# The low parts of the first three query weights are subtracted on GpSimd in place of VectorE

## What is computed

```
x  = x + g1 * _rms(mix_x @ w_out, norm_post_mix)
h2 = _modulate(_rms(x, norm_pre_ffn), sh2, sc2)
q  = h2 @ peer_w_query              # 512 x 1024 @ 1024 x 2048
s1 = q[..., :128] @ keys1.T         # per head; s2 with the other half
v1, i1 = top_k(s1, 16) ...          # candidates, top 16 of 256, softmax
out = x + g2 * _rms(sum over the picked experts of gelu(h2 . u) * v, norm_post_ffn)
```

## Time and profile before

| | us |
|---|---|
| median of 3 runs | 1504.64 (1502.85 to 1504.99) |
| the profiled execution | 1502.96 |
| its span | 1501.2 |
| PE busy | 1479.3 (99%) |
| DVE busy | 1242.2 (83%) |
| ACT busy | 578.0 (39%) |
| POOL busy | 438.7 (29%) |

### The profile page before, as it was taken

One profiled execution on the slowest core, in us unless ns is written; L12 is line 12 of the kernel. 1 busy time (PEld: TensorE's weight loads), 2 busy tenths in 40 slices (PEclk: granted clock), 3 DMA queues, 4 the chain that ended last, 5 costly groups with the idle time before them and its releaser, 6 DMA issues.

```text
span 1501.2 us, 21716 instructions
## 1 busy us (share of the span) xinstructions
PE 1479.3 (99%) x8085; PEld 1305.6 (87%) x8085; DVE 1242.2 (83%) x2364; ACT 578.0 (39%) x869; POOL 438.7 (29%) x373
## 2 busy tenths in 40 slices
PE   8999999999999999999999999999999999999998
PEld 3887888788999999999999999988888888888886
DVE  3888758776899998999999955698888888888886
ACT  4432143622333334344444443343333333333333
POOL 1130000010578886432222201322222222222210
PEclk9999999999999999999999999999999999999999
DMA  9775113134358896799999999999999999999983
GB/s 387 267 285 183 57 57 112 43 98 155 135 197 303 288 312 216 264 337 359 372 363 372 371 324 353 388 412 363 377 354 379 386 369 381 385 362 368 367 320 129
DMA packets 149158, 433.49 MB, mean 289 GB/s; under 512 B 13408, under 2 KB 46432, under 8 KB 146272
## 3 DMA queue, kind: packets, MB, share of 16 engines
q1 hardware_dynamic: 73296, 203.91, 37.2%
q0 software_dynamic: 42048, 153.11, 27.9%
q10 hardware_dynamic: 33744, 75.64, 13.3%
HBM read 378.08 MB, written 54.53 MB: 288 GB/s over the span
## 4 chain that ended last, share of the span: by engine, by line
PE 73%; DVE 19%; DMA 3%; issue 2%; ACT 1%; POOL 0%; SPq 0%; ACTq 0%; DVEq 0%
PE ps L1688 22%; PE ps L1690 22%; PE ps L1689 22%; PE ps L2078 3%; DVE rows L1485 2%; DMA part_w<-w_ada 2%; DMA ada_w<-w_ada 2%; DVE part_acc L1114 1%; DVE ps L1517 1%; DVE ps L1521 1%; DVE picks L1523 1%; PE ps L2018 1%; DVE tv L1451 1%; DVE tv L1454 1%; DVE ws_lo L1081 1%
## 5 line engine op out<-in xcount | busy, mean ns | idle before, releaser
L1688 PE MATMUL ps<-hT_hi,ws_hi 128*128 128x384 f32 (+1 forms) x976 | 341.2, 350 | 2.7 <-POOL ws_lo L632 1.5
L1690 PE MATMUL ps<-hT_hi,ws_lo 128*128 128x384 f32 (+1 forms) x976 | 335.2, 343 | 0.0
L1689 PE MATMUL ps<-hT_lo,ws_hi 128*128 128x384 f32 (+1 forms) x976 | 335.1, 343 | 0.0
L1688 PE MATMUL ps<-vs_hi,coef_hi 128*128 128x512 f32 x768 | 299.0, 389 | 0.8 <-DVE coef_lo L1647 0.8
L1690 PE MATMUL ps<-vs_hi,coef_lo 128*128 128x512 f32 x768 | 298.8, 389 | 0.0
L1689 PE MATMUL ps<-vs_lo,coef_hi 128*128 128x512 f32 x768 | 298.8, 389 | 0.0
L970 ACT ACTIVATE vs_hi<-blk_raw 128x1024 fp32r<-128x1024 f32 x128 | 135.7, 1060 | 284.8 <-PE ps L1690 282.2
L640 POOL DMA_INDIRECT rows<-u_nat,ids x128 | 142.7, 1115 | 300.6 <-DVE sp_act L1485 293.0
L640 POOL DMA_INDIRECT rows<-v_nat,ids x128 | 127.1, 993 | 332.2 <-DVE ps L1605 300.4
L1644 DVE TENSOR_TENSOR vs_lo<-blk_raw,vs_hi 128x1024 fp32r<-128x1024 f32 x128 | 156.6, 1224 | 67.7 <-ACT vs_hi L970 66.7
L916 ACT ACTIVATE ws_hi<-blk_raw 128x1024 fp32r<-128x1024 f32 x102 | 108.1, 1060 | 245.9 <-PE ps L1690 242.4
(11 more groups left out here) (319 smaller groups left out, 2232.0 us busy)
## 6 DMA issues: line engine op xcount, KB each, us to landing
blk_raw<-u_t SPq DMA_DIRECT2D x128, 512.0 KB, 5.8
blk_raw<-v_nat SPq DMA_DIRECT2D x128, 512.0 KB, 7.1
g_dram<-g_buf ACTq DMA_DIRECT2D x128, 192.0 KB, 4.9
w_dram<-w_stage SPq DMA_DIRECT2D x48, 512.0 KB, 8.5
grp_g<-g_dram ACTq DMA_DIRECT2D x15, 1536.0 KB, 9.9
grp_w<-w_dram ACTq DMA_DIRECT2D x15, 1536.0 KB, 25.8
part_w<-w_ada POOLq DMA_DIRECT2D x32, 512.0 KB, 5.9
raw<-w_in SPq DMA_DIRECT2D x20, 512.0 KB, 6.6
```

What stands on the lines that cost most here:

```text
L1688: pe.matmul(o, lh, rh, start=start, stop=False, skip_group_check=True)
L1689: pe.matmul(o, lh, rl, start=False, stop=False, skip_group_check=True)
L1690: return pe.matmul(o, ll, rh, start=False, stop=stop, skip_group_check=True)
```

## The change

Units 28, 29 and 30 have their low parts subtracted on GpSimd. The three calls of `rest_unit` on DVE are gone. GpSimd gets three subtractions, each behind a wait for the rounded high part and for the count of low parts before it; they stand behind the memsets and ahead of `apply_gain(2, ...)`. DVE gets one wait, ahead of `rest_unit(31)`, for the third of them, so that the count stays in order.

```diff
+POOL_UNITS = (28, 29, 30)
...
+            for n in POOL_UNITS:
+                pool.wait_ge(split_hi, n + 1)
+                pool.wait_ge(split_lo, n)
+                pool.tensor_tensor(ws_lo[slot(n)][:], raw[:, n % RAW, :], ws_hi[slot(n)][:].bitcast(F32),
+                                   ALU.subtract).then_inc(split_lo, 1)
             pool.wait_ge(split_used, 31)
             pool.wait_ge(gg_step, 4)
             apply_gain(2, gg_last)
...
-                if tb >= 2:
-                    rest_unit(26 + tb)
                 sum_x(tb)
...
-                if m == 3:
-                    rest_unit(30)
...
             dve.wait_ge(gg_step, 4)
             for m in range(2 * PH):
+                if m == 3:
+                    dve.wait_ge(split_lo, POOL_UNITS[-1] + 1)
                 if m >= 3:
                     rest_unit(28 + m)
                     take_pair(m - 3)
```

## The result

The changed kernel takes 1506.03 us in the median, the kernel before, run beside it, 1502.66 us (18 runs each; the three runs known before gave 1504.64). The ratio is 1.0023 with a 95% interval of 1.0016 to 1.0031, so the kernel became 2.4 to 4.7 us slower; 3.8 us was forecast. One disturbed execution of the changed kernel (2111 us, mean granted clock 0.654) and one of the kernel before in a later set (2870 us) are left out of the comparisons; the median of the other 17 is 1505.94 us.

The account below looks back on a forecast made before the run. The bound was taken as the chain of waits ending on PE (73%) and DVE (19%), with PE waiting for the normalization. 1.1 + 1.95 + 0.75 = 3.8 us on 1504.64 gave 1508.4, range 1506.0 to 1511.2.

Parts of the forecast that it names:

- the holds: Between 270 and 290 us, DVE instructions with two SBUF inputs wait until POOL's subtraction ends; 3.8 us in sum.
- the clock: Rival: PE's clock falls to 1.2 GHz in a 3.6 us gap before the matmul of ones, 2.3 us more; chance 0.14.
- What DVE is rid of: Three subtractions of 1.22 us leave DVE, mostly covered by other waits; gain 0.1 + 0.1 + 0.2 = 0.4 us.
- PE's stall: PE waits shortly before 288.77 for the low part of tile 2, behind the third subtraction; taken as 0.2 us.
- Unit 28: In block 2, POOL's subtraction holds DVE's 128x1 sum of squares until POOL ends at 276.7; +1.1 us.
- Unit 29: In block 3, POOL gets in between the halves of x and holds the second; +1.95 us.
- The rival in which POOL comes behind it: In block 3, POOL starts only after the second half of x; total 2.95 us, time 1507.6; chance 0.12.
- the row of 407.36: Earlier trace's POOL row that got in between two DVE instructions, 0.07 ahead of the next; nearest case for unit 29.
- Unit 30: POOL holds the first `hT_lo` subtraction, PE starts 0.95 later, its stall of 0.2 goes; +0.75 us.
- The shift reaches the end in full: A shift of the first query matmul, at 285.60, counts in full as a shift of the kernel's end.
- The rule of the port pair: VectorE and GpSimd share an exclusive lock, taken by a two-SBUF-input VectorE instruction or a GpSimd one for its whole length.
- a view of shared bandwidth: The two engines only share bandwidth, so DVE would have no such waits and the sum would be a 0.4 us gain.

Follow-up runs that it names:

- e5_tiny: Kernel before, with the subtractions of units 28, 29 and 30 cut from 1024 columns to 1 on VectorE, nothing on GpSimd; ratio to before 0.9997.
- e8_late30: Kernel before, with unit 30's subtraction on VectorE moved from the third tile to behind the eighth; ratio to before 0.9998.
- e1_after_fed: Changed kernel with 16 matmuls of ones added on PE between the early transposes and the first keep_clock matmul; ratio to before 1.0036.
- e4_only29: Changed kernel, but only unit 29 is subtracted on GpSimd, units 28 and 30 stay on VectorE; ratio to before 1.0015.
- e10_one_input: Changed kernel with the 128x1 sum of squares on DVE written with one tensor input and a pointer scalar; ratio to before 1.0027.
- e6_pieces: Changed kernel with each of the three GpSimd subtractions cut into eight of 128 columns; ratio to before 1.0002.
- e9_window: Against the kernel before: unit 29 alone on GpSimd, behind the last scaled x, and unit 30 on VectorE behind the eight tiles; ratio 0.9997.
- e3_only28: Changed kernel, but only unit 28 is subtracted on GpSimd, units 29 and 30 stay on VectorE; ratio to before 1.0007.
- fed gaps: 16 matmuls of ones in PE's gap, added to the changed kernel (1.0036) and to before with unit 29 subtracted three times on VectorE (1.0023; unfed 1.0024).

## Why the prediction was right

- **Direction and size.** Forecast +3.8 us, measured +3.4 (2.4 to 4.7). The time of 1506.03 lies 2.4 us under the forecast 1508.4 and only 0.03 above the lower end of the range, 1506.0. 2.0 of the 2.4 us are the starting point: before measured 1502.66 in more runs, not 1504.64. That the absolute time still fell inside the range is luck; the difference is what was forecast well. A little luck is in that too: at an equal clock the holds are worth 3.2 us by the estimate above, and falls of the clock, which the sum left out, add some 0.3.
- **What DVE is rid of**, put at 0.1 + 0.1 + 0.2: `e5_tiny` shows 0.21 in the first interval and 0.44 in the second, and `e8_late30` 0.23 for PE's stall. Right, because DVE would have waited for ACT anyway: in `e5_tiny` it waits 0.88 and 0.87 us ahead of the two sums.
- **Unit 28**, put at +1.1 with the sum ending with POOL: 1.05.
- **Unit 29**, put at +1.95 with POOL getting in between the halves of x: 1.84, with the second half at 2.84 us. The rival in which POOL comes behind it did not happen in any of the four traces with this pair (changed, `e1_after_fed`, `e4_only29`, `e10_one_input`): the POOL rows start 0.11 to 0.12 us ahead of the held half (279.84 and 279.96). The close call was decided by the row of 407.36, and rightly.
- **Unit 30**, put at +0.75: 0.88 less 0.22, that is 0.66.
- **The shift reaches the end in full**: 5.30 us at the transposes, 5.35 at the end.
- **The rule of the port pair** (the Trainium skill, SBUF — State Buffer, "SBUF: two separate sides"), weighed against a view of shared bandwidth: `e6_pieces` decides for the lock, since the same bytes in eight instructions hold DVE for 0.1 to 0.3 us at a time where one held it for 0.9 to 2.1. `e9_window` and `e10_one_input` show its other side, which instructions pass.
- **Where it fell short: the clock.** I gave its fall 0.14 and went by one trace, in which a gap of 2.14 us had left the clock alone; my expectation for `e3_only28` took shorter gaps as safe. Two runs show otherwise. In `e3_only28` the clock fell behind a gap of 1.94 us, and in `e8_late30` it fell in a part that is as before, when PE had begun again after the gap of the earlier trace rows:

```profile
132.76 0.47 PE L1792 MATMUL ps<-up_hi,tab_hi 128*128 128x512 f32 x1 [2.09 <-DVE up_lo L1228]
...
133.30:136.70 3.40, 3.40 (x9) 2.67 (x8) 2.12 (x10) 1.66 (x7) 0.00 (x0) 0.50 0.59 213
```

  So low stretches belong to code that the change leaves alone too, and the change made them more frequent (0.9982 against 0.9989). In the profiled execution of the changed kernel the rival came true beside the forecast: a fall of 6.8 us that cost 1.7. The price that I had put on it was 2.3, from the first 5 us of the kernel, taken as a stretch at the low clock. The rows don't show that: the earlier trace rows have a granted clock of 1.00 there as in the next 5 us. On average over the runs the falls cost far less, some 0.3 us by the estimate above; the pairs with and without fed gaps don't differ beyond their intervals.

The Trainium skill (TensorE: Matmul & The Clock Gate, Part 1) ties the clock to how busy the engine has been. The traces agree in kind: every low stretch found here began in an idle stretch of PE (2.16 us into it in `e10_one_input`) or at most 1.4 us behind one, and the two fed gaps had none. They don't show a length of gap from which it falls: it fell behind 1.87 us (`e1_after_fed`, at 31 us) and not behind 3.45 (`e4_only29`).

## What to carry to other kernels

Before an elementwise instruction moves from VectorE to GpSimd, look at what VectorE runs beside it: each GpSimd subtraction here held back the VectorE instruction with two SBUF inputs that came while it ran, even one of 128x1, until it had ended. If the held one is a link of a chain, all that is left of the GpSimd instruction's length comes onto the chain (0.9 to 1.8 us of 2.4 here). It was harmless beside instructions that read PSUM, and nearly so when it was cut into short pieces. And first ask what the work costs where it is: three times 1.22 us of busy VectorE were worth 0.4 us.

## What was not expected of the hardware

- A sum of 128x1 with two SBUF tensor inputs waits for GpSimd (1.32 us), the same sum with one tensor input and a pointer scalar in SBUF does not (0.21 us). With one input, casts of 128x8 and 128x128 wait, and MAX8 on 128x128 and a reciprocal of 128x1 don't; these runs don't show what sets them apart.
- GpSimd's subtraction of 128x1024 takes 2.35 to 2.41 us in one piece and 4.24 us in eight. Two of the eight took 0.87 and 0.90 us, the others 0.45 each, 0.42 apart; with all eight like these it would be 3.4 us, so each further instruction costs about 0.14 us, and the two longer ones, which stood beside DVE's instructions, the rest (an estimate from these rows).
- PE's granted clock can fall while PE is working again, 1.4 us (284.52 to 285.9) after the end of a gap of 3.77 us, and it doesn't fall in each execution with such a gap.
